# Attended values of a hybrid decoder layer: float32r from split operands in place of float32

## What is computed

```python
def rms_norm(x, g):
    xf = x.astype(jnp.float32)
    y = xf * lax.rsqrt(jnp.mean(xf * xf, axis=-1, keepdims=True) + EPS)
    return (y * g.astype(jnp.float32)).astype(x.dtype)
...
def swa_sink_attention(q, k, v, sinks):
    bn, s, _ = q.shape
    nb = s // BLOCK
    qb = q.reshape(bn, nb, BLOCK, N_KV_HEADS, GQA_GROUP, HEAD_DIM)
    kb = k.reshape(bn, nb, BLOCK, N_KV_HEADS, HEAD_DIM)
    vb = v.reshape(bn, nb, BLOCK, N_KV_HEADS, HEAD_DIM)
    pad = ((0, 0), (1, 0), (0, 0), (0, 0), (0, 0))
    kk = jnp.concatenate([jnp.pad(kb, pad)[:, :nb], kb], axis=2)
    vv = jnp.concatenate([jnp.pad(vb, pad)[:, :nb], vb], axis=2)
    scores = jnp.einsum('bnqhgd,bnkhd->bnhgqk', qb, kk,
                        preferred_element_type=jnp.float32) * (HEAD_DIM ** -0.5)
    ...
    mask = (diff >= 0) & (diff < WINDOW) & (kpos >= 0)
    scores = jnp.where(mask[None, :, None, None, :, :], scores, NEG_INF)
    ...
    probs = jax.nn.softmax(jnp.concatenate([scores, sink], axis=-1), axis=-1)[..., :2 * BLOCK]
    out = jnp.einsum('bnhgqk,bnkhd->bnqhgd', probs.astype(vv.dtype), vv)
    return out.reshape(bn, s, Q_WIDTH)
...
    h = rms_norm(x, norm_mix_pre[l])
    proj = jnp.einsum('bsd,de->bse', h, w_in[l])
    u_pool, g_b, g_c, u_conv, q, k, v = jnp.split(proj, offsets, axis=-1)
    y_pool = pool_mixer(u_pool, pool_w[l], pool_scale[l])
    y_conv = g_b * causal_dwconv(g_c * u_conv, conv_w[l])
    y_attn = swa_sink_attention(q, k, v, attn_sinks[l])
    mix = jnp.einsum('bse,ed->bsd', jnp.concatenate([y_pool, y_conv, y_attn], axis=-1), w_o[l])
    x = x + rms_norm(mix, norm_mix_post[l])
    h = rms_norm(x, norm_ffn_pre[l])
    up = causal_dwconv(jnp.einsum('bsd,df->bsf', h, ffn_w_up[l]), ffn_conv_w[l]) + ffn_conv_b[l]
    gate, val = jnp.split(up, 2, axis=-1)
    ff = jnp.einsum('bsf,fd->bsd', jax.nn.silu(gate) * val, ffn_w_down[l])
    x = x + rms_norm(ff, norm_ffn_post[l])
```

## Time and profile before

| what | us |
|---|---|
| three runs, lowest, median, highest | 955.59, 955.65, 955.72 |
| the profiled execution | 955.72 |
| its span in the trace | 953.9 |
| PE busy | 943.0 |
| DVE busy | 656.3 |
| ACT busy | 434.1 |
| POOL busy | 187.5 |

### The profile page before, as it was taken

One profiled execution on the slowest core, in us unless ns is written; L12 is line 12 of the kernel. 1 busy time (PEld: TensorE's weight loads), 2 busy tenths in 40 slices (PEclk: granted clock), 3 DMA queues, 4 the chain that ended last, 5 costly groups with the idle time before them and its releaser, 6 DMA issues.

```text
span 953.9 us, 11489 instructions
## 1 busy us (share of the span) xinstructions
PE 943.0 (99%) x4419; PEld 776.3 (81%) x4419; DVE 656.3 (69%) x710; ACT 434.1 (46%) x648; POOL 187.5 (20%) x182
## 2 busy tenths in 40 slices
PE   8999999999999999999999999999999999999997
PEld 7988777778888887888888888888888888888886
DVE  6545786666755899777877787778776653535668
ACT  5524444445433455444544454445444454335352
POOL 2301000000111424234222434353431100000021
PEclk9999999999999999999999999999999999999999
DMA  6999981005322236476443355555546775677555
GB/s 223 269 335 208 214 148 45 23 23 177 133 89 89 89 88 199 143 161 186 129 145 108 118 126 130 124 119 124 134 99 194 202 241 204 232 273 253 179 163 199
DMA packets 114248, 151.16 MB, mean 158 GB/s; under 512 B 6289, under 2 KB 66193, under 8 KB 114193
## 3 DMA queue, kind: packets, MB, share of 16 engines
q1 hardware_dynamic: 100737, 118.63, 38.3%
q0 software_dynamic: 13456, 31.79, 16.7%
HBM read 113.17 MB, written 60.29 MB: 182 GB/s over the span
## 4 chain that ended last, share of the span: by engine, by line
PE 92%; DVE 4%; ACT 1%; POOL 1%; issue 1%; DVEq 0%; POOLq 0%; ACTq 0%
PE ps L1609 28%; PE ps L1611 28%; PE ps L1610 28%; PE ps L1619 1%; PE ps L1744 1%; PE ps L1767 1%; PE ps L1745 1%; PE ps L1753 1%; POOL w_sums L684 1%; PE ps L1670 1%; DVE r_lo L1374 1%; PE ps L1771 1%; DVE h2lo L1370 1%; PE ps L1782 0%; DVE wraw L1382 0%
## 5 line engine op out<-in xcount | busy, mean ns | idle before, releaser
L1609 PE MATMUL ps<-hhi,whi 128*128 128x512 f32 (+1 forms) x240 | 91.1, 380 | 0.5 <-DVE hlo L1135 0.5
L1611 PE MATMUL ps<-hhi,wlo 128*128 128x512 f32 (+1 forms) x240 | 88.5, 369 | 0.0
L1610 PE MATMUL ps<-hlo,whi 128*128 128x512 f32 (+1 forms) x240 | 88.5, 369 | 0.0
L684 POOL TENSOR_TENSOR w_sums<-wraw 128x1024 f32<-128x1024 f32 x20 | 48.1, 2406 | 190.5 <-DVE w2lo L1370 62.1
L646 POOL TENSOR_SCALAR meansq<-sumsq 128x1 f32<-128x1 f32 x28 | 10.0, 357 | 374.6 <-ACT yg L1039 170.8
L998 ACT ACTIVATE yg<-ps,par_b 128x1024 f32<-128x1024 f32 x21 | 25.3, 1207 | 60.2 <-DVE ps L1496 60.2
L1609 PEld LDWEIGHTS ps<-hhi,whi 128*128 128x128 f32 x240 | 45.3, 189 | 8.0 <-DVE hlo L1135 0.7
L1611 PEld LDWEIGHTS ps<-hhi,wlo 128*128 128x128 f32 x240 | 45.2, 189 | 7.6
L1610 PEld LDWEIGHTS ps<-hlo,whi 128*128 128x128 f32 x240 | 45.3, 189 | 7.4 <-issue 0.5
L1444 DVE SCALAR_TENSOR_TENSOR yg<-ps,par_a,yg 128x1023 f32<-128x1023 f32 x22 | 28.2, 1282 | 26.7 <-ACT yg L998 26.7
L1609 PE MATMUL ps<-h2hi,whi 128*128 128x512 f32 x116 | 45.4, 391 | 0.2 <-DVE wraw L1145 0.2
(11 more groups left out here) (261 smaller groups left out, 2710.4 us busy)
## 6 DMA issues: line engine op xcount, KB each, us to landing
wraw<-in_ffn_w_up SPq DMA_DIRECT2D x42, 512.0 KB, 5.2
s_dram<-in_ffn_w_down POOLq DMA_DIRECT2D x6, 2816.0 KB, 27.9
wraw<-r_dram SPq DMA_DIRECT2D x44, 256.0 KB, 3.7
wraw<-s_dram SPq DMA_DIRECT2D x44, 256.0 KB, 4.6
r_dram<-cst SPq DMA_DIRECT2D x33, 256.0 KB, 2.8
wraw<-act_dram SPq DMA_DIRECT2D x33, 256.0 KB, 3.6
wraw<-in_ffn_w_down SPq DMA_DIRECT2D x33, 256.0 KB, 4.6
wraw<-in_w_in SPq DMA_DIRECT2D x14, 512.0 KB, 10.8
```

The costliest lines, as they stand in the source:

```text
L684: pool.tensor_tensor(w_sums[:, 0:2, :], raw[:, 0:4:3, :], raw[:, 2:3, :].broadcast_to([P, 2, HALF]), ALU.add)\
L1609: pe.matmul(acc, w_hi, x_hi, start=first, stop=False, skip_group_check=looped)
L1610: pe.matmul(acc, w_hi, x_lo, start=False, stop=False, skip_group_check=looped)
L1611: return pe.matmul(acc, w_lo, x_hi, start=False, stop=last, skip_group_check=looped)
```

## The change

It computes the attended values in float32r. The turned probabilities P are taken unmasked from PSUM: ACT rounds them to `p_parts[0]` (`round_probs`), and DVE writes the rest to `p_parts[1]`. The values of one head (64 channels) are rounded and split too, and rounded values and rest stand side by side as one weight of 128 columns (`values`). With V' the values of the block before and V those of the own block, the kernel now computes V' P + (V - V') (P masked to the own block). So one mask is left, over both parts at once (`own_parts`, 1024 columns), and the values' change V - V' is made by DVE in place in `v_tok` and split in its turn. In block 0 there is no block before: V takes the place of V', and the second product is left out.

A unit has four matmuls of 512 columns (two in block 0). Partitions 0 to 63 of bank 7 get the products of the rounded values, 64 to 127 those of the rests. They have to be added: ACT copies the upper half to `mix_att` in two pieces, since two heads lie on other partitions there, and DVE adds the lower half to it in two pieces (`sum_attended`). The exponentials are now made in place in `s_sb`, so `prob` is gone, and `mhi_even` and `gain_b` change places in memory.

```diff
-        prob = alloc(xb_, "prob", [P, 2, 4, P])
-        pt_cur = alloc(xb_, "pt_cur", [P, 4, P])
-        pt_prev = alloc(xb_, "pt_prev", [P, 4, P])
+        p_parts = alloc(xb_, "p_parts", [P, 2, 4, P], F32R)
+        own_parts = alloc(xb_, "own_parts", [P, 2, 4, P], F32R)
...
+        values = alloc(xv, "values", [P, 2, 4, HD], F32R)
...
+        mhi_even = alloc(xc, "mhi_even", [P, KD, P], F32R)
         gain_b = alloc(xc, "gain_b", [P, DM])
-        mhi_even = alloc(xc, "mhi_even", [P, KD, P], F32R)
...
+        def value_of(u, ahead):
+            b, kv = UNIT[u]
+            return v_tok[:, max(b - 1, 0) if ahead else b, kv * HD:(kv + 1) * HD]
...
             def copy_scores(u):
                 act.wait_ge(scored, u + 1)
+                if u >= 2:
+                    act.wait_ge(p_turned, u - 1)
                 act.activation(s_sb[:, u % 2, :, :], score_view[:, :, 1, :], ACT.Copy)\
                    .then_inc(s_copied, 1)
             def exps(u):
                 act.wait_ge(negmax, u + 1)
-                if u >= 2:
-                    act.wait_ge(p_turned, u - 1)
                 for i in range(4):
-                    act.activation(prob[:, u % 2, i, :], s_sb[:, u % 2, i, :], ACT.Exp,
+                    act.activation(s_sb[:, u % 2, i, :], s_sb[:, u % 2, i, :], ACT.Exp,
                                    bias=small[:, u % 2, 1, i:i + 1], scale=QK_SCALE,
                                    accum_out=small[:, u % 2, 3, i:i + 1])
                 act.activation(small[:, u % 2, 4, :], small[:, u % 2, 2, :], ACT.Exp)\
                    .then_inc(expd, 1)
+            def round_values(u):
+                act.wait_ge(vt_ready, 1)
+                if u >= 2:
+                    act.wait_ge(pv_done, u - 1)
+                if u >= 1:
+                    act.wait_ge(change_made, behind_one(u - 1))
+                act.activation(values[:, u % 2, 0, :], value_of(u, True), ACT.Copy)\
+                   .then_inc(value_hi, 1)
+            def round_change(u):
+                if UNIT[u][0]:
+                    act.wait_ge(change_made, behind_one(u))
+                    act.activation(values[:, u % 2, 2, :], value_of(u, True), ACT.Copy)\
+                       .then_inc(change_hi, 1)
+            def round_probs(u):
+                act.wait_ge(p_turned, u + 1)
+                if u >= 1:
+                    act.wait_ge(pv_done, u)
+                act.activation(p_parts[:, 0, :, :], ps[:, 6, :].rearrange("p (h q) -> p h q", h=4),
+                               ACT.Copy).then_inc(p_rounded, 1)
...
             def copy_attended(u):
                 act.wait_ge(pv_done, u + 1)
                 b, kv = UNIT[u]
-                act.activation(mix_att[:, b, kv, 0:2, :].rearrange("p k c -> p (k c)"),
-                               ps[:, 7, 0:2 * P], ACT.Copy).then_inc(pv_out, 1)
+                for e in range(2):
+                    last = act.activation(mix_att[e * HD:(e + 1) * HD, b, kv, 0:2, :]
+                                          .rearrange("p k c -> p (k c)"),
+                                          ps[HD:P, 7, e * 2 * P:(e + 1) * 2 * P], ACT.Copy)
+                last.then_inc(rest_out, 1)
...
                 copy_scores(u)
+                round_values(u)
+                if u >= 1:
+                    round_probs(u - 1)
...
                 exps(u)
+                round_change(u)
...
             copy_attended(UNITS - 2)
+            round_probs(UNITS - 1)
             start_conv(1)
...
             def mask_probs(u):
-                dve.wait_ge(p_turned, u + 1)
-                if u >= 1:
+                dve.wait_ge(p_rounded, u + 1)
+                dve.tensor_tensor(p_parts[:, 1, :, :], ps[:, 6, :].rearrange("p (h q) -> p h q", h=4),
+                                  p_parts[:, 0, :, :], ALU.subtract).then_inc(p_split, 1)
+                if UNIT[u][0]:
                     dve.wait_ge(pv_done, u)
-                turned_p = ps[:, 6, :].rearrange("p (h q) -> p h q", h=4)
-                last = dve.tensor_tensor(pt_cur[:, :, :], turned_p, over_heads(cur_ok), ALU.mult)
+                    dve.wait_ge(p_split, u + 1)
+                    dve.tensor_tensor(own_parts[:, :, :, :].rearrange("p x h q -> p (x h) q"),
+                                      p_parts[:, :, :, :].rearrange("p x h q -> p (x h) q"),
+                                      cur_ok.rearrange("p (o j) -> p o j", o=1)
+                                      .broadcast_to([P, 8, P]), ALU.mult).then_inc(p_masked, 1)
+            def sum_attended(u):
+                dve.wait_ge(rest_out, u + 1)
+                b, kv = UNIT[u]
+                for e in range(2):
+                    out = mix_att[e * HD:(e + 1) * HD, b, kv, 0:2, :].rearrange("p k c -> p (k c)")
+                    last = dve.tensor_tensor(out, ps[0:HD, 7, e * 2 * P:(e + 1) * 2 * P], out, ALU.add)
+                last.then_inc(pv_out, 1)
+            def low_values(u):
+                dve.wait_ge(value_hi, u + 1)
+                dve.tensor_tensor(values[:, u % 2, 1, :], value_of(u, True),
+                                  values[:, u % 2, 0, :], ALU.subtract).then_inc(value_lo, 1)
                 if UNIT[u][0]:
-                    last = dve.tensor_tensor(pt_prev[:, :, :], turned_p, over_heads(prev_ok),
-                                             ALU.mult)
-                last.then_inc(p_masked, 1)
+                    dve.wait_ge(value_lo, u + 1)
+                    dve.tensor_tensor(value_of(u, True), value_of(u, False), value_of(u, True),
+                                      ALU.subtract).then_inc(change_made, 1)
+            def low_change(u):
+                if UNIT[u][0]:
+                    dve.wait_ge(change_hi, behind_one(u))
+                    dve.tensor_tensor(values[:, u % 2, 3, :], value_of(u, True),
+                                      values[:, u % 2, 2, :], ALU.subtract).then_inc(change_lo, 1)
...
                     mask_probs(u - 1)
+                    low_change(u - 1)
+                if u >= 2:
+                    sum_attended(u - 2)
+                low_values(u)
...
             mask_probs(UNITS - 1)
+            low_change(UNITS - 1)
+            sum_attended(UNITS - 2)
             conv_taps(1)
...
                     low_wo(0)
                     low_mix(1)
+                    sum_attended(UNITS - 1)
...
             def attend(u):
                 b, kv = UNIT[u]
-                pe.wait_ge(p_masked, u + 1)
-                if u == 0:
-                    pe.wait_ge(vt_ready, 1)
+                pe.wait_ge(p_split, u + 1)
+                pe.wait_ge(value_lo, u + 1)
+                if b:
+                    pe.wait_ge(p_masked, behind_one(u))
+                    pe.wait_ge(change_lo, behind_one(u))
                 if u >= 1:
                     pe.wait_ge(pv_out, u)
-                cols = slice(kv * HD, (kv + 1) * HD)
-                for e in range(2):
-                    acc = ps[e * HD:(e + 1) * HD, 7, 0:2 * P]
-                    heads = slice(2 * e, 2 * e + 2)
-                    last = pe.matmul(acc, v_tok[:, b, cols],
-                                     pt_cur[:, heads, :].rearrange("p h q -> p (h q)"),
-                                     start=True, stop=b == 0)
-                    if b:
-                        last = pe.matmul(acc, v_tok[:, b - 1, cols],
-                                         pt_prev[:, heads, :].rearrange("p h q -> p (h q)"),
-                                         start=False, stop=True)
+                products = [(0, p_parts, 0), (0, p_parts, 1)]
+                if b:
+                    products += [(2, own_parts, 0), (2, own_parts, 1)]
+                for n, (kind, parts, rest) in enumerate(products):
+                    last = pe.matmul(ps[:, 7, :], values[:, u % 2, kind:kind + 2, :]
+                                     .rearrange("p x c -> p (x c)"),
+                                     parts[:, rest, :, :].rearrange("p h q -> p (h q)"),
+                                     start=n == 0, stop=n == len(products) - 1)
                 last.then_inc(pv_done, 1)
```

More of the change, by code:

```diff
@@ L176, in build @@
         xb_.close()
+        xv = ExitStack()
+        alloc(xv, "under_values", [P, 6 * DM + 3 * (PAD + SEQ) + 3 * P])
+        values = alloc(xv, "values", [P, 2, 4, HD], F32R)
+        xv.close()
         xb2 = ExitStack()
@@ L380, in turn_banks, with behind_one @@
             return (4 + 2 * (i % 2) if i < NT else 2 + 4 * (i % 2)), 2
+        def behind_one(u):
+            return sum(1 for b, _ in UNIT[:u + 1] if b)
+        def value_of(u, ahead):
+            b, kv = UNIT[u]
+            return v_tok[:, max(b - 1, 0) if ahead else b, kv * HD:(kv + 1) * HD]
         def wo_bank(t):
@@ L1250, in norm_probs @@
                 finish_step(dve.reciprocal(small[:, u % 2, 0, :], small[:, u % 2, 5, :]))
[L1251 removed]
+                p = s_sb[:, u % 2, :, :]
                 dve.tensor_tensor(p, p, over_keys(small[:, u % 2, 0, :]), ALU.mult)\
```

17 lines of the change are left out of this document (12 added, 5 removed).

## The result

The changed kernel takes **973.88 us** (median of 5 runs, 973.12 to 974.87), the kernel before 955.69 on the same chip. The ratio is 1.019, with a 95% interval of 1.0179 to 1.0201: slower by 18.2 us. The forecast was 967.0, with a range up to 971.0. The sign was right and the time lies 2.9 us above the range.

A forecast was written before the change was run, and what follows sets the result against it. The prediction took PE, busy 943.0 of 953.9 us, to bound the kernel. Stage stalls +12.6, tail +3.9 and PE's gain -4.9 sum to +11.6 on 955.72: 967.3, rounded to 967.0 us, range 961.0 to 971.0.

The forecast's parts named there:

- PE's gain: Attended values on PE: four float32r matmuls cost 0.91 us instead of 1.21, giving 0.30 per unit, -4.9 us over 16.
- DVE's price: Attention stage: DVE work per unit rises from 1.20 to 3.26 us, +2.06, with the two additions not overlapping.
- Rivals 1: Attention stage: extra DVE work is hidden and PE's gain stands; 951 to 957 us, chance 0.10.
- rival 2: Attention stage: additions and mask both come out cheap, half the overrun; 957.6 to 961 us, chance 0.07.
- rival 3: Attended values: PE gives nothing back, the four matmuls take 1.2 us as before; 969 us, chance 0.07.
- Rival 4: Dearer hand-overs (0.1 us) and short instructions (0.29 for 64 columns) together; +16, 972 us, chance 0.08.
- The slots: Attention stage, stretches from one unit's scores to the next's: DVE lateness stalls PE, +12.6 us in all, 4.0 in slot 9.
- Only 0.38 us of lateness is free: Attended matmuls: DVE's operands are ready at T+6.5 (T: scores' start), PE comes at T+6.87; before, the margin was 2.1 us.
- no idle time between 105 and 155: Attention stage: a sign of the forecast being right, DVE never idle between about 105 and 155 us.
- The tail: Output projection: unit 15's addition delays the last gate product by 2.9 us, later DVE adds 1.0; +3.9 us.
- any stall put into it lengthens it one for one: Whole kernel: PE's instructions are the program's clock, so each PE stall adds exactly its own length.
- a plain shift: Behind the attention stage: the following stage moves later as a whole, with the stalls changing nothing else there.

The follow-up runs named there:

- Experiments 1: The changed kernel with idle matmuls (results never read) filling PE's three longest stalls: 969.33 us, ratio 1.0143.
- 2: The kernel before with three idle DVE instructions ahead of the second gate product, pausing PE: 961.45 us; with 15 idle matmuls filling that pause: 959.26 us.
- first form of experiment 7: The changed kernel with own-block masks, values' rests and change on GpSimd, last addition behind the third following weight rest, ScalarE's order unchanged: 957.53 us, ratio 1.0016.

## Why the prediction was wrong

- **PE's gain, 0.30 per unit, -4.9:** right. Alone it gave a span shorter by 4.9, 0.3 of it by an earlier start, and 0.3 less in each interval.
- **DVE's price, 2.06 more per unit:** right, each part within 0.06 but for the values' change in slot 2, and the two additions do not overlap (0.87 for the pair). Rivals 1 and 2 fall with this, and rival 3 with the gain. (The 957.6 to 961 of rival 2 does not follow from its own 1.7 to 4 us, which give 957.4 to 959.7; nothing hangs on it.) Rival 4's 972 is the nearest number to the result, but not for its reason: the hand-over did cost 0.1, the 64 columns 0.13 to 0.26 and not 0.29 throughout, and the loss over the forecast is mostly the clock.
- **The slots:** right place by place, within 0.3 each. "Only 0.38 us of lateness is free" held: every later mask of scores showed up as a wait. One sign did not come: DVE was to have no idle time between 105 and 155, but it idles 3.07 us ahead of 111.10, waiting for the score copy.
- **The tail, 3.9:** 0.5 too small without the clock. The rounding of w_o rows on ACT and the addition stand as forecast; the page shows 4.02 of wait, and the slip is 4.4.
- **The step that failed** is the very first one, "any stall put into it lengthens it one for one", with "at full granted clock" read off the kernel before and carried over to a kernel with pauses. The clock is no constant of the kernel. Three pauses of 1.68, 3.95 and 4.02 us cost 5.6 us more than their length, 3.1 in the stage and 2.5 behind the output projection, where a plain shift was assumed. Experiments 1 and 2 show it by filling the same pauses, and 2 shows it in the kernel before. The Trainium skill, "TensorE: Matmul & The Clock Gate", Part 1, says that an idle stretch of TensorE takes its clock back to half; the trace agrees for these three pauses (0.83, 0.83, 0.69), though not for every pause of the length of the first, as the last section shows. With a sum that itself forecast two pauses of 4 us, the clock should have been a term of it.
- **Small terms:** the stalls cost 1.4 us more than forecast over all, 0.5 of it in the tail and 0.3 in slot 3, inside the bounds given. The hand-over from subtraction to mask, 0.1 and not 0.04, is one part of that.

With the clock's term, known only afterwards, the sum would have been 967.3 + 5.6 = 972.9, and with the 1.4 it is the 974.3 of the profiled run; the median is 973.88.

## What to carry to other kernels

When a forecast puts pauses into a TensorE that now runs without any, price each pause at its length plus about 0.2 us, and for the longer ones add the matmuls that then run at half clock: here 1.3 us for a pause of 2.5, 2.7 for one of 3.0, and 1.6 to 2.9 for 3.7 to 4.0; one of 1.7 cost either 1.5 or nothing. These prices are a range and not a rule of the length: the same kernel had executions with and without a fall. Before moving work from TensorE to VectorE to gain 0.3 us per unit, look at the margin between VectorE's result and TensorE's arrival (0.38 us here), not at the average share. And when VectorE has become the scarce engine, look at what it waits for itself: one ScalarE copy in the wrong place cost 4.2 us of the 18, 2.6 of waiting and 1.6 of clock.

## What the hardware showed beyond that

- **TensorE's clock after a pause.** It is not a matter of the pause's length alone: in the profiled executions 1.68 us brought a fall in slot 3 in three kernels and none in a fourth, while 1.88 and 1.80 us at other places (attended values of slot 9 with GpSimd's masks, and turn 11) brought none. Where it falls, it stays at 1.2 GHz for 3.3 to 6.1 us, and it need not begin with the pause's end: with a pause of 2.5 it began two products later, and in slot 3 of the kernel after six score matmuls run at full pace first. Idle matmuls prevented it in all four pauses in which they were tried.
- **VectorE and GpSimd hold each other up.** With the masks on POOL (first form of experiment 7), DVE's and POOL's timelines:

```profile
178.76 1.16 DVE L1329 TENSOR_TENSOR small<-small,sinks 128x4 f32<-128x4 f32 x1
```
```profile
178.58 1.32 POOL L710 TENSOR_TENSOR own_parts<-p_parts,cst 128x512 fp32r<-128x512 f32 x1 [0.62 <-ACT p_parts L903]
```

A VectorE instruction on 128x4 that takes 0.16 us elsewhere takes 1.16 and ends at 179.92, as GpSimd's mask does at 179.90. The other way round, GpSimd's rest of 128x64, 0.32 alone, takes 1.22 at 144.70 while VectorE has a weight rest of 1.65 (1.22 alone). The Trainium skill, "SBUF — State Buffer", section "SBUF: two separate sides", calls this an exclusive lock that goes to whoever starts first, for a VectorE instruction with two SBUF inputs as here; the rows agree. GpSimd's half mask costs 1.30 us where VectorE's whole one costs 1.14; the trade paid all the same, since GpSimd was idle.
